# Moving the second half's row preparation behind each early step's reads, and loading the first head's values earlier

## The reference, cut to what matters

```python
def hybrid_layer(hid, norm_pre_w, w_in, ...):
    u = rms_norm(hid, norm_pre_w)                      # (1, 2048, 1024)
    proj = jnp.einsum('bsd,de->bse', u, w_in)          # 1024 -> 6672 columns
    q, k, v, g_attn, z, xbc, dt_raw = jnp.split(proj, ...)
    attn = mixture_of_dilations(q, k, v) * silu(g_attn)
    xbc = silu(causal_depthwise_conv(xbc, conv_w, conv_b))
    y = ssd_chunked(...) + d_skip * xs
    y = gated_group_rms_norm(y, z, ssm_norm_w)
    out = jnp.einsum('bse,ed->bsd', concat([attn, y]), w_out)
    return hid + rms_norm(out, norm_post_w)
```

## Time and profile before

| | |
|---|---|
| median of 3 runs | 2245.77 us (2244.99 to 2254.86) |
| the profiled execution, its own time | 2247.01 us |
| its span in the trace | 2245.3 us |
| mean granted TensorE clock | 0.982 of full speed |
| TensorE busy | 2147.4 us (96%) |
| VectorE, ScalarE, GpSimd busy | 1370.1, 1028.2, 1444.0 us |
| `project` | from 0 to about 1133 us |
| `attend` | from about 1134 to 1726 us |

### The profile page before, as it was taken

The page is one execution under the profiler, slowest core; times in us unless marked ns, Lnnn a source line. Parts: engine busy times, 40 slices in busy tenths (PEclk is TensorE's granted clock), DMA queues, the critical chain, the costliest instruction groups (busy, mean ns, idle before and its releaser), DMA issues. The chain is left out here.

```text
span 2245.3 us, 34807 instructions
## 1 busy us (share of the span) xinstructions
PE 2147.4 (96%) x12061; PEld 1830.6 (82%) x12061; DVE 1370.1 (61%) x2581; ACT 1028.2 (46%) x2365; POOL 1444.0 (64%) x877
## 2 busy tenths in 40 slices
PE   5999999999999999999979999999995899999998
PEld 3778888888888888888759999999994688888886
DVE  7556666344656665234467777777777767666661
ACT  5334444343434343334348777777773423232231
POOL 5678888778688888677625565664642456555552
PEclk9999999999999999999989999999997799999999
DMA  3552333334533333333355656556556244444431
GB/s 124 200 195 76 115 111 125 102 103 138 189 104 104 121 114 115 102 94 113 94 122 130 152 142 149 116 137 158 138 156 230 80 143 136 131 136 129 134 101 57
DMA packets 260221, 287.20 MB, mean 128 GB/s; under 512 B 78420, under 2 KB 228112, under 8 KB 251984
## 3 DMA queue, kind: packets, MB, share of 16 engines
q1 hardware_dynamic: 258944, 277.50, 41.9%
q0 software_dynamic: 1104, 7.47, 0.8%
HBM read 195.28 MB, written 81.00 MB: 123 GB/s over the span
## 5 line engine op out<-in xcount | busy, mean ns | idle before, releaser
L968 PE MATMUL mm<-b_hi,w_hi 128*128 128x512 f32 x1456 | 572.5, 393 | 6.6 <-DVE fm L799 5.1
L970 PE MATMUL mm<-b_hi,w_lo 128*128 128x512 f32 x1456 | 568.2, 390 | 0.0
L969 PE MATMUL mm<-b_lo,w_hi 128*128 128x512 f32 x1456 | 567.7, 390 | 0.0
L527 POOL TENSOR_TENSOR w_lo<-w_raw,w_hi 128x512 fp32r<-128x512 f32 x208 | 298.9, 1445 | 76.0 <-ACT w_hi L601 68.4
L968 PEld LDWEIGHTS mm<-b_hi,w_hi 128*128 128x128 f32 x1456 | 274.0, 188 | 64.7 <-issue 9.2
L970 PEld LDWEIGHTS mm<-b_hi,w_lo 128*128 128x128 f32 x1456 | 274.0, 188 | 57.7
L969 PEld LDWEIGHTS mm<-b_lo,w_hi 128*128 128x128 f32 x1456 | 274.2, 188 | 55.6
L601 ACT ACTIVATE w_hi<-w_raw 128x512 fp32r<-128x512 f32 x208 | 130.8, 629 | 254.0 <-PE mm L970 233.9
L1772 PE MATMUL ps_t<-ident_b,probs 128*128 128x128 f32 x1136 | 213.8, 278 | 7.5 <-ACT probs L1699 5.7
L2257 PE MATMUL ps_out<-wo_hi,mix_hi 128*128 128x512 f32 x512 | 208.1, 406 | 1.3 <-ACT mix_hi L2208 1.3
L799 DVE SCALAR_TENSOR_TENSOR fm<-mm,u 128x512 f32<-128x512 f32 x120 | 92.5, 771 | 189.8 <-PE mm L970 189.6
(11 more groups left out here) (242 smaller groups left out, 4450.2 us busy)
## 6 DMA issues: line engine op xcount, KB each, us to landing
w_raw<-in_w_in_dram SPq DMA_DIRECT2D x52, 1024.0 KB, 5.3
feat<-fm SPq DMA_DIRECT2D x56, 512.0 KB, 5.3
tok<-tok_tile SPq DMA_DIRECT2D x52, 512.0 KB, 3.7
raw_q<-feat SPq DMA_DIRECT2D x32, 512.0 KB, 6.4
raw_k<-feat SPq DMA_DIRECT2D x32, 512.0 KB, 6.4
cum_b<-cum_scratch SPq DMA_DIRECT2D x16, 1024.0 KB, 7.5
cls_nat<-cls_out SPq DMA_DIRECT2D x64, 132.0 KB, 2.7
v_cls<-tok SPq DMA_DIRECT2D x64, 128.0 KB, 3.6
```

The costliest lines, as they stand in the source:

```text
L527: pool.tensor_tensor(wl[o][:, :, :], source(o, n), wh[o][:, :, :].bitcast(F32), ALU.subtract)\
L968: pe.matmul(bank, w_hi[:, k, :], bh[o][:, k, :], start=(opens and k == 0), stop=False)
L969: pe.matmul(bank, w_hi[:, k, :], bl[o][:, k, :], start=False, stop=False)
L970: last = pe.matmul(bank, w_lo[:, k, :], bh[o][:, k, :], start=False, stop=(closes and k == KH - 1))
```

## The change

Two things are changed.

1. In steps 0 to 3, the preparation of the second half's rows moves to the end of the step. ScalarE's two squares go from the start of the step to behind the high half of weight part S1 (`high(4, n + 1)`). VectorE's first `normalise` goes to just before the step's last read (S4), its second one and the four sums to just behind it. Before, all of it stood around the first read of the step (S2). SyncE's order in these steps stays as it was.
2. The values of head 0 get tiles of their own, placed in `FirstHead` where the second half's operands T2 lie in `project`. SyncE loads them at the end of `project`, when product S2 of the last step is over and all token stores have landed. In `attend` they are no longer loaded; q and k of head 1 move up.

```diff
@@ project, SyncE, behind the last step
+                for b in range(2):
+                    sp.wait_ge(tok_out[b], 16 * turns)
+                sp.wait_ge(product, PRODUCTS * LAST + T2 + 1)
+                for dst, part in v_loads(dram["tok"], first.v_nat, first.v_cls, 0):
+                    sp.dma_start(dst, part).then_inc(first.v_in, 16)
                 sp.wait_ge(gated, 2 * gates)
@@ project, ScalarE
                 for s in steps:
                     n = s.n
-                    if n in PREP:
-                        for half in range(2):
-                            square(HT + 2 * PREP[n] + half)
...
                     high(4, n + 1)
+                    if n in PREP:
+                        for half in range(2):
+                            square(HT + 2 * PREP[n] + half)
@@ project, VectorE
-                    if n in PREP:
-                        for half in range(2):
-                            normalise(HT + 2 * PREP[n] + half)
...
                     read(s, S2, u2[:, :], c1[:, :])
-                    if n in PREP:
-                        late_sums(PREP[n])
...
                     dve.wait_ge(dve_read, READS * n + 5)
+                    if n in PREP:
+                        normalise(HT + 2 * PREP[n])
                     read(s, S4, put(s, 0, 1), u2[:, :])
+                    if n in PREP:
+                        normalise(HT + 2 * PREP[n] + 1)
+                        late_sums(PREP[n])
@@ attend, SyncE
+                    if not is_int(head, 0):
+                        for dst, part in v_loads(tok, v_nat[b], v_cls[b], head):
+                            sp.dma_start(dst, part).then_inc(v_in[b], 16)
```

More of the change, by code:

```diff
@@ L98, in __init__ @@
         self.k_rest = place(nc, "k_rest0", TANH_AT, [P, SEQ], F32R)
+        self.v_nat = place(nc, "v_nat0", EARLY_END, [P, TT, HEAD_DIM])
+        self.v_cls = place(nc, "v_cls0", EARLY_END + 4 * KB, [P, TT, HEAD_DIM])
         spare = Rooms(nc, MASKS_AT, TINY_AT)
@@ L112, in __init__ @@
         self.q_sorted = sem("q_sorted")
+        self.v_in = sem("v_in0")
         self.dt_out = sem("dt_out")
@@ L165, in all_steps, with v_loads @@
     return out
+def v_loads(tok, v_nat, v_cls, head):
+    cols = slice(head * HEAD_DIM + V_COL, (head + 1) * HEAD_DIM + V_COL)
+    by_class = tok.rearrange("(n i c) f -> c i n f", n=CLASS_BLOCKS, c=CLASSES)
+    natural = tok.rearrange("(n i c) f -> c i n f", i=SHARE, c=CLASSES)
+    out = [(v_cls[:, c * CLASS_BLOCKS:(c + 1) * CLASS_BLOCKS, :], by_class[c][:, :, cols]) for c in range(CLASSES)]
+    return out + [(v_nat[c * SHARE:(c + 1) * SHARE, :, :], natural[c][:, :, cols]) for c in range(CLASSES)]
 def project(nc, dram, first, x, norm_pre_w, w_in, conv_w, conv_b):
@@ L1165, in attend @@
         sb = Rooms(nc, EARLY_END, W1_AT)
-        v_nat, v_cls = [sb("v_nat0", [P, TT, HEAD_DIM])], [sb("v_cls0", [P, CLASS_UNITS, HEAD_DIM])]
-        assert sb.at == SEG_END
+        v_nat, v_cls = [first.v_nat], [first.v_cls]
+        sb.at = SEG_END
         v_nat.append(sb("v_nat1", [P, TT, HEAD_DIM]))
@@ L1211, in attend @@
         made, raw_in, high_made, split, q_sorted = first.made, first.raw_in, first.high_made, first.split, first.q_sorted
-        v_in = [sem(f"v_in{b}") for b in range(2)]
+        v_in = [first.v_in, sem("v_in1")]
         g_in = sem("g_in")
@@ L1367, in _ @@
                 feat, tok = dram["feat"], dram["tok"]
-                v_by_class = tok.rearrange("(n i c) f -> c i n f", n=CLASS_BLOCKS, c=CLASSES)
-                v_natural = tok.rearrange("(n i c) f -> c i n f", i=SHARE, c=CLASSES)
                 def load_qk(head, which="qk"):
```

## The result

The changed kernel takes 2285.0 us, median of 4 runs (2282.4 to 2286.5), against 2247.6 for the kernel before on the same chip. The ratio is 1.0159, 95% interval 1.0146 to 1.0173: 1.6% slower. The forecast was 2269 with a range up to 2277, so its direction holds and its size does not: the loss is 37 us where 23 were forecast (2269 was counted from the median of 2245.8 that was known then). The profiled execution has a span of 2283.7 us against 2245.3, that is +38.4, and a mean granted clock of 0.971.

A forecast was written before the change was run, and what follows sets the result against it. TensorE, busy 96%, was taken as the bound, with a rows' loop pacing steps 0 to 3. 2247.0 + 30 (rows) - 7 (values) = 2270, less 1.2 for the median: 2268.8, say 2269; range 2257 to 2277.

The forecast's parts named there:

- Where the loss comes from: Steps 1 to 3: TensorE waits 8 to 11 us before S4, for A12 reads held by the fm store.
- The loop's length: Steps 0 to 3, from row stores to the next: 31.0 us a turn instead of 21.7.
- row stores to row loads: SyncE's queue, steps 0 to 3: 6.5 us from issuing row stores to issuing row loads.
- row loads to the A12 read: SyncE's queue: 11.4 us from row loads to the fm store's landing, which the A12 read needs.
- A12 read to the sums' end: VectorE: 13.0 us for reads to A22, normalise, S4 read, normalise and sums of 6.2.
- the forecast of 87.6: Step 0: the row sums are ready at 87.6 us, against 75.5 before.
- Step 4: Store wait 6.5, memsets and S2 read 0.9, A22 and S4 5.4: last read at 193.4 us, against 163.44.
- At unit 5 the gain: In attend, ScalarE gets head 1's q 7 us earlier, bounds 4.3 and 9.0.
- the loop's bound of 32.5 us: Upper bound of a turn in steps 0 to 3; with it the rows' move costs +34 us.
- Rival 1: Project: fm store lands early and stays out of the loop, which stays at 21.7 us; 2242 us, chance 6%.
- Rival 4: Attend: early values give nothing, ScalarE waits for q until the same time; 2276 us, chance 6%.
- Rival 3: Steps' end: sums run clear of GpSimd, 3.4 us less for each of four; 2255 us, chance 6%.

The follow-up runs named there:

- only the squares back: Changed kernel with only ScalarE's two squares back at the start of the step: 2281.0 us, ratio 1.0136.
- part 2 alone: Kernel before with head 0's values loaded at the end of project, rows prepared where they were: 2245.8 us, ratio 0.9978.
- the fastest kernel: Changed kernel; fm store first, normalises ahead of S4 read, row loads awaiting row tiles alone, step 4 memsets behind S2 read, step 3 sums stored first: 2236.9 us.
- The kernel with the store first: Changed kernel with each step's fm store issued ahead of the row stores and row loads in steps 0 to 3: 2253.7 us, ratio 1.0017.
- the kernel with the store between stores and loads: Kernel before with values early, sums behind A12 and S3 reads, row loads awaiting row tiles alone, fm store between row stores and loads: 2252.1 us.
- part 1 alone: Changed kernel with head 0's values loaded in attend as before, rows still moved: 2291.1 us, ratio 1.0185.
- its version without part 2: The fastest kernel with head 0's values loaded in attend again: 2241.3 us, ratio 0.9965.

## Why the prediction was right or wrong

**Where the loss comes from: right.** TensorE's three waits before S4, released by an A12 read that itself waits for `feat<-fm`, the row stores moving apart, the shorter wait in step 4: all of it is in the trace. The waits are 11.8 to 14.0 us, where 8 to 11 were forecast. The store's place was the cause, which was argued before and is now shown: moving only that takes 31 of the 37 us away.

**The loop's length: wrong by 2.6 to 4.2 us a turn, three times.** Its three terms, forecast and measured:

| term | forecast | turns 1, 2, 3 |
|---|---|---|
| row stores to row loads | 6.5 | 6.5, 5.9, 5.9 |
| row loads to the A12 read | 11.4 | 13.0, 11.4, 11.6 |
| A12 read to the sums' end | 13.0 | 15.7, 16.2, 16.3 |

The step that failed is the third term, from the A12 read to the end of the sums, "the sums 6.2: 13.0 us". It is 3.1 us short in the mean, in three pieces. VectorE waited 1.2 to 1.7 us for product S4, made at 1.2 GHz after each stall; the prediction named this ("up to 1.6 us later"), put it into the upper bound, and left it out of the value taken, though the earlier trace rows showed the low clock behind a wait of only 2.75 us. The second normalise took 2.34 us, not the 1.28 of the earlier trace rows: it was priced by a row in which GpSimd stood idle, while in its new place GpSimd has just begun (its rows are in the last section). The trace of the kernel before had the other price as well, in step 0, where GpSimd began 0.07 us ahead of it:

```profile
66.42 2.30 DVE L757 SCALAR_TENSOR_TENSOR tok_tile<-tok_tile,stat,fm 128x1024 f32<-128x1024 f32 x1
```

```profile
66.35 1.29 POOL L527 TENSOR_TENSOR w_lo<-w_raw,w_hi 128x512 fp32r<-128x512 f32 x1 [2.03 <-ACT w_hi L601]
```

And the sums took 6.7, not 6.2: all four of them lie beside GpSimd now, where the first one took 1.19 in the earlier trace rows. Had the prediction carried its own argument on the sums ("GpSimd's next parts start at 81.49") over to the normalise ahead of them, it would have had another 1 us a turn. In turn 1 the second term has 1.6 us more. The weight load ahead of the `fm` store is late there too: it landed 9.6 us after its issue, against 8.0 and 8.2 in the next turns. The time-step columns' store behind it can't be the reason by itself: the kernel before and the one with only the squares back have it at the same place, and there the term is 11.4. The cause stays open.

At step 0 the same two errors, the normalise and the sums, were covered by a start that was 1.3 us early. Of this 1.1 was there before anything that the change moved, so the forecast of 87.6 was met by luck.

**Step 4: 2.1 us short.** The memsets began 6.7 us after the last stores (6.5 forecast), but from there to the last read it was 8.2, not 6.3, since TensorE came out of its wait at 1.2 GHz again (granted clock 0.62 from 198 to 202 us). With the loop's 9.5 and 0.4 at step 0 this makes the 11.9 us by which the last read came later, 205.33 against 193.4.

**Part 2: the wait for the values went, the size was somewhat high.** At unit 5 the gain is 6.0, where 7 was taken: q was issued when forecast, but landed after 8.0 us and not 7.1. What the prediction didn't have is what TensorE waits for next. It named the small loads as a wait of VectorE "as before", but ScalarE stands for them too, and its `probs` come after: TensorE's first product with the values started 9.4 us earlier, counted from the start of `attend`, and the new wait of 3.5 us takes that down to about 6, ahead of q and by another way. All `attend` together, its waits for `probs` are 9.1 us instead of 5.7; in the kernel with part 2 alone they are 10.4. By the end of `attend` 4.0 are left (+37.84 at the first load of `cum_b`, against +41.85 at the start), and 3.5 by the end of the span. Some of what is given back is seen: the small loads come 1.3 us later relative to the start of `attend` (VectorE's wait is 3.50 us instead of 1.93), and TensorE had a stretch at 0.50 from 1208 to 1212 us. The runs say rather more than the profiles: 5 us alone, 6 beside part 1, 4 to 7 in the fastest kernel. The forecast's bounds, 4.3 and 9, hold for nearly all of these.

**The sum.** 2268.8 + 11.9 + 3.5 = 2284, against 2285.0. The range failed with it. Its upper end took the loop's bound of 32.5 us, and the loop was 34.2 in the mean: the bound was made of one of the three missing pieces alone.

**The rivals.** None took place. Rival 1 has the store out of the loop. The kernel with the store first makes it so, and even there its time of 2242 was too low, by 12 us in the median and 8 in the ratio. It took the rows' loop to stay at 21.7, but the loop grew to 22.2 to 24.1 and its end now lay 12 us nearer to step 4, where the memsets wait for it. Rival 4, no gain from part 2, is ruled out by part 2 alone. Rival 3 was wrong in its sign: work moved to the step's end ran more beside GpSimd, not clear of it.

## What to carry to other kernels

When a step is moved later, look on every in-order queue for what stands behind what it releases: here the moved sums held a store that had nothing to do with them. Price each operation of a newly closed loop in its new company, with the engine it shares time with busy and the clock at the level a stall leaves behind; such terms are paid once per turn. And a loop that is taken away uncovers the next one: the move paid off beyond part 2 only when three waits had gone, each found in the profile of the kernel with the one before it removed.

## What the runs showed of the hardware

- A store of one tile of 128x1024 on SyncE's queue, issued in pairs, landed 3.1 us after its issue (median) with nothing queued ahead of it, 6.1 right behind the row stores (the kernel with the store between stores and loads), and 9.4 behind row loads and 1 MB of weights.
- VectorE's normalise, 128x1024 with two inputs in SBUF, took 1.28 us with GpSimd idle or when it began first (at 76.07; GpSimd's operation from 76.57 then took 1.93), and 2.05 to 2.34 us where GpSimd had begun an operation ahead of it. GpSimd's timeline in the changed kernel, beside the normalise of 2.34 us from 78.79 and the first sum from 81.17:

```profile
78.76 1.30 POOL L545 TENSOR_TENSOR w_lo<-s_two,w_hi 128x512 fp32r<-128x512 f32 x1 [0.25 <-ACT w_hi L619]
80.20 2.09 POOL L529 TENSOR_TENSOR s_one<-w_raw 128x512 f32<-128x512 f32 x1
```

  They take turns. GpSimd is first at 78.76 and takes 1.30, its normal time; the normalise begins 0.03 later and needs 1.28 more than the time until 80.06, less 0.2. GpSimd's next operation begins while the normalise still runs and takes 2.09 instead of 1.29. The Trainium skill (SBUF — State Buffer, Who interferes with whom) calls the port pair that the two engines share an exclusive lock, says that a VectorE instruction with two inputs in SBUF contends there with GpSimd's reads, and that issue order decides who blocks; these rows agree.
- The stage after `attend` has a place whose length changes by 2.6 us between kernels that differ only ahead of it. Between two `cum_b` loads it took 28.2 us in before and in the changed kernel and 30.9 in the one with part 2 alone, and also in the one with part 1 alone. With part 2 alone TensorE's clock was 0.50 from 1775 to 1780 us, after a wait of 4.9 us; in the kernel before the same wait was 2.95 us, and the clock was 1.00 behind it. In the fastest kernel's profile the 2.7 us are lost too, and in that of its version without part 2 they are not: their spans differ by only 0.5 us, where the runs have 4 to 7. Whether the state of that place varies from run to run stays open.
